# Thirty-two modulation tiles of layer two taken from TensorE's products to VectorE's multiply-and-sum

## The reference, cut to what matters

```
modulate(t, shift, scale) = t * (1.0 + scale) + shift
mod = silu(c) @ ada_w[layer] + ada_b[layer]      # six vectors of 1024 per layer
```

## Time and profile before

| | us |
|---|---|
| median of three runs | 1952.42 |
| the profiled execution | 1952.34 |
| its span, from the first to the last instruction | 1950.6 |
| TensorE busy | 1773.7 (91%) |
| VectorE busy | 823.5 (42%) |
| ScalarE busy | 355.2 (18%) |

### The profile page before, as it was taken

The page is one execution under the profiler, slowest core; times in us unless marked ns, Lnnn a source line. Parts: engine busy times, 40 slices in busy tenths (PEclk is TensorE's granted clock), DMA queues, the critical chain, the costliest instruction groups (busy, mean ns, idle before and its releaser), DMA issues.

```text
span 1950.6 us, 33854 instructions
## 1 busy us (share of the span) xinstructions
PE 1773.7 (91%) x14556; PEld 1372.6 (70%) x14556; DVE 823.5 (42%) x1796; ACT 355.2 (18%) x853; POOL 0.2 (0%) x4
## 2 busy tenths in 40 slices
PE   8999999999999999999999999999999766666666
PEld 4456644888888886777788887878788644555545
DVE  1355535766667325444444413268433111111112
ACT  0233313211110003222211102112332000000002
POOL 0000000000000000000000000000000000000000
PEclk9999999999999999999999999899999988988889
DMA  9455642222221305112333543132376999999996
GB/s 372 178 217 225 256 151 83 87 86 86 86 102 60 119 33 151 65 65 76 130 130 134 226 163 146 65 130 74 143 288 258 419 427 429 429 428 429 429 429 278
DMA packets 30925, 394.10 MB, mean 202 GB/s; under 512 B 3440, under 2 KB 6512, under 8 KB 8176
## 3 DMA queue, kind: packets, MB, share of 16 engines
q1 hardware_dynamic: 30832, 392.74, 50.2%
HBM read 391.68 MB, written 1.05 MB: 201 GB/s over the span
## 4 chain that ended last, share of the span: by engine, by line
PE 78%; DMA 19%; DVE 2%; ACT 1%; issue 1%; SPq 0%; DVEq 0%
PE bank L498 23%; DMA ring<-w_moe 18%; PE bank L1673 13%; PE bank L551 8%; PE bank L1405 6%; PE bank L1886 3%; PE bank L3103 2%; PE bank L783 2%; PE bank L694 2%; PE bank L1882 1%; PE bank L1080 1%; PE bank L2221 1%; PE bank L1284 1%; PE bank L1920 1%; PE bank L1056 1%; PE bank L1938 1%
## 5 line engine op out<-in xcount | busy, mean ns | idle before, releaser
L498 PE MATMUL bank<-layer_input,ring 128*128 128x256 f32 x1152 | 257.2, 384 | 1.1 <-DVE arena L2481 1.1
L498 PEld LDWEIGHTS bank<-layer_input,ring 128*128 128x128 f32 x1152 | 220.1, 193 | 34.1 <-issue 3.0
L3103 PE MATMUL bank<-ring,arena 128*32 128x128 f32 x1920 | 77.0, 327 | 55.7 <-DMA ring<-w_moe 55.4
L1673 PE MATMUL bank<-arena 128*128 128x256 f32 x504 | 115.6, 379 | 0.0
L3103 PEld LDWEIGHTS bank<-ring,arena 128*32 128x32 f32 x1920 | 66.0, 132 | 68.1 <-DMA ring<-w_moe 66.2
L1405 PE MATMUL bank<-arena,ring 128*128 128x256 f32 x480 | 107.0, 380 | 1.4 <-ACT arena L1496 1.4
L3220 DVE TENSOR_TENSOR arena<-arena,bank 128x128 f32<-128x128 f32 x32 | 9.2, 288 | 227.4 <-PE bank L3103 227.4
L1673 PEld LDWEIGHTS bank<-arena 128*128 128x128 f32 x504 | 95.8, 190 | 13.0
L1405 PEld LDWEIGHTS bank<-arena,ring 128*128 128x128 f32 x480 | 90.7, 190 | 15.4 <-ACT arena L1496 2.8
L551 PE MATMUL bank<-arena,ring 128*128 128x256 f32 x452 | 99.1, 380 | 0.8 <-DVE arena L2031 0.6
L551 PEld LDWEIGHTS bank<-arena,ring 128*128 128x128 f32 x452 | 85.5, 190 | 13.3 <-issue 1.0
(11 more groups left out here) (469 smaller groups left out, 2641.3 us busy)
## 6 DMA issues: line engine op xcount, KB each, us to landing
arena<-w_moe SPq DMA_DIRECT2D x46, 2048.0 KB, 26.5
ring<-w_moe SPq DMA_DIRECT2D x45, 2048.0 KB, 25.8
ring<-w_ffn_in SPq DMA_DIRECT2D x22, 2048.0 KB, 7.8
ring<-w_ada_late SPq DMA_DIRECT2D x16, 2560.0 KB, 10.4
ring<-w_ffn_out SPq DMA_DIRECT2D x8, 2816.0 KB, 9.5
ring<-w_proj SPq DMA_DIRECT2D x7, 3072.0 KB, 9.9
ring<-w_na_pair SPq DMA_DIRECT2D x8, 1536.0 KB, 6.5
arena<-w_ada_far SPq DMA_DIRECT2D x2, 2048.0 KB, 25.1
```

Source lines behind the costliest of these rows:

```text
L498: last = pe.matmul(out, a, b, start=(k == 0), stop=(k == len(lhs) - 1))
L1673: last = pe.matmul(out, w[:, k * P:(k + 1) * P], x[:, k, :], start=(start and k == 0), stop=(stop and k == 3), skip_group_check=True)
L3103: ins = eng.matmul(bank[x][group[q], 0:P], xe[:, k, SLOTS * e:SLOTS * e + SLOTS], weight(e, last, (x * KT + k) * FE + q * P, P), start=(k ...
```

## The change

- `ada_late` becomes 8 chunks of 6 tiles (before: 16 of 5), 48 tiles instead of 80. TensorE makes them in the MLA heads in one piece a pair, cut in two: the first 4 (even pair) or 5 (odd pair) of the eight slices k between `project` and `turn`, the rest between `turn` and `attend`. VectorE turns and adds the piece once a pair, behind the copies of `turned`.
- The last 32 tiles (gate of the attention, and shift, scale and gate of the feed-forward part, of layer two) are made by VectorE in the neighbourhood heads, for the latent column. For each tile one `tensor_tensor_reduce` over 128 partitions by 1024 elements multiplies the weights, laid out with the outputs on the partitions, by `silu(c)` repeated on all partitions, sums, and adds `ada_b`. The pairs take 0, 4, 4, 4, 5, 5, 5, 5 tiles; four stand between `normalize` and `na_turned`, a fifth behind `na_turned`.
- SP loads `c` (0.5 MB, repeated on 128 partitions) and sixteen chunks of 1 MB with two tiles each, through three buffers, between the pairs' weights. ScalarE applies `Silu` to the repeated `c` at the end of pair 0.
- At the end of the MLA heads one of three small additions of 1 to a scale vector is replaced by a memset; the addition is made at the start of `na_out`.

```diff
@@ -95,19 +95,24 @@
 VALUE_W = 768
 
 
-ADA_FIRST, ADA_TILES = 4 * 4, 5
+ADA_FIRST, ADA_TILES, ADA_CHUNKS = 4 * 4, 6, 8
+FAR_FIRST = ADA_FIRST + ADA_TILES * ADA_CHUNKS
+FAR_BUFFERS, FAR_EACH = 3, 2
+FAR_PER_PAIR = (0, 4, 4, 4, 5, 5, 5, 5)
+FAR_TILES = sum(FAR_PER_PAIR)
+FAR_LOADS = FAR_TILES // FAR_EACH
 MLA_PAIRS, MLA_QUADS = MLA_H // 2, MLA_H // 4
 MLA_QP = MLA_PAIRS * (QLT + KVT)
 OPEN_GROUPS = ((0, 1), (1, 2), (2, 4), (4, 6), (6, 8))
 OPEN_AT = ((0, 0, 2048), (0, 2048, 4096), (1, 0, 4096), (2, 0, 4096), (3, 0, 4096))
 STREAM = [("ada", 2, KT * 512), ("mla_v", 1, KVT * D),
-          ("ada_late", 16, KT * ADA_TILES * P), ("mla_o", 2, 4096),
+          ("ada_late", ADA_CHUNKS, KT * ADA_TILES * P), ("mla_o", 2, 4096),
           ("ffn_in0", 11, 4096), ("ffn_out0", 4, 5632),
           ("na_pair", NA_PAIRS, 3072), ("na_o", 2, 4096),
           ("ffn_in1", 11, 4096), ("ffn_out1", 4, 5632),
           ("proj", 7, 6144), ("branch", 1, 4096), ("w_out", 2, 4096),
           ("moe", EXPERTS, (2 * KT + 2 * FET) * FE), ("cmp", 1, 4096), ("branch_hg", 1, 4096), ("mla_qk", 1, (MLA_QP + MLA_QUADS * QLT) * P),
-          ("ada_far", 2, KT * 512), ("mla_in", 2, 3 * D)]
+          ("ada_far", 2, KT * 512), ("mla_in", 2, 3 * D), ("far", FAR_LOADS, FAR_EACH * D), ("far_c", 1, D)]
 UPS = 2 * KT * FE
 RESIDENT = EXPERTS - QUAD
 LAST = EXPERTS - 1
@@ -322,6 +327,9 @@
                 if name == "na_pair" and first == 1:
                     sp.wait_ge(self.sem("ffn0_up_used"), FT + 4)
                     self.load_biases(sp, slice(4, 16), self.rest_in)
+                    self.load_pairs(sp, load, g0)
+                    first = n
+                    break
                 first += 1
             sem, upto = CHUNK_USED[name]
             turns = (n - first) // 2
@@ -346,6 +354,37 @@
             sp.wait_ge(self.sem(ready), 1)
             sp.dma_start(out[:, t, :], self.result()[:, t, :]).then_inc(self.sem("result_out"), 16)
         sp.wait_ge(self.sem("result_out"), 32)
+
+    def far_c(self):
+
+        return self.ring[0][:, 4096:4096 + D]
+
+    def far_weights(self, b):
+
+        w = FAR_EACH * D
+        return self.B[:, 6400 + b * w:6400 + (b + 1) * w] if b < 2 else self.ring[1][:, 4096:4096 + w]
+
+    def load_far(self, sp, i):
+
+        b = i % FAR_BUFFERS
+        if i >= FAR_BUFFERS:
+            sp.wait_ge(self.sem("ada_used"), len(OPEN_GROUPS) + FAR_EACH * (i - FAR_BUFFERS + 1))
+        sp.dma_start(self.far_weights(b), self.W["far"][i]).then_inc(self.sem(f"far_in{b}"), 16)
+
+    def load_pairs(self, sp, load, g0):
+
+        sp.dma_start(self.far_c(), self.W["far_c"][0]).then_inc(self.cvec_in, 16)
+        for i in range(FAR_BUFFERS):
+            self.load_far(sp, i)
+        i, used = FAR_BUFFERS, 0
+        for u in range(NA_PAIRS):
+            if u + RING < NA_PAIRS:
+                sp.wait_ge(self.sem("na_proj_done"), u + 1)
+                load(u + RING, (g0 + u) % 2, g0 + u + RING)
+            used += FAR_PER_PAIR[u]
+            while i < min(FAR_LOADS, used // FAR_EACH + FAR_BUFFERS):
+                self.load_far(sp, i)
+                i += 1
 
     def load_biases(self, sp, heads, loaded):
         biases = self.N[:, :].rearrange("p (t h k) -> p t h k", t=2, h=16)
@@ -685,11 +724,11 @@
 
         return self.X[:, 3712:3712 + 32 * KT].rearrange("p (k c) -> p k c", k=KT)
 
-    def ada_product(self, pe, out, weights, width):
+    def ada_product(self, pe, out, weights, width, inner=(0, KT)):
 
         cs = self.silu()
         n = width // 4
-        for k in range(KT):
+        for k in range(*inner):
             for g in range(4):
                 last = pe.matmul(out[32 * g:32 * g + 32, 0:n], cs[:, k, :],
                                  weights[:, k * width + g * n:k * width + (g + 1) * n],
@@ -714,7 +753,8 @@
     def ada_rest(self, who, eng):
 
         if who == "dve":
-            for layer, m in ((0, 4), (1, 1), (1, 4)):
+            eng.memset(self.ADA[:, 1, 2 * KT:, :], 0.0)
+            for layer, m in ((0, 4), (1, 1)):
                 sc = self.ADA[:, layer, m * KT:(m + 1) * KT, :]
                 self.link(eng, who, eng.tensor_scalar(sc, sc, 1.0, None, ALU.add))
 
@@ -958,7 +998,7 @@
                 order += [("qp", n // 2)] * fresh + [("qn", n), ("kn", n)]
                 order += [("swap", n // 2), ("rot", n // 2)] * fresh
             if u >= 0:
-                order += [("ada", 2 * u), ("ada", 2 * u + 1), ("av", u)]
+                order += [("ada", u), ("av", u)]
         return {x: r for r, x in enumerate(order)}
 
     def mla_heads(self, who, eng):
@@ -1026,11 +1066,16 @@
             if n % 2 == 0:
                 rotate(n // 2)
 
-        def ada(c):
-            g = FIRST["ada_late"] + c
-            pe.wait_ge(self.w_loaded[g % 2], 16 * (g // 2 + 1))
-            b = claim(("ada", c))
-            self.ada_product(pe, b, self.ring[g % 2], ADA_TILES * P).then_inc(s["ada_rows"], 1)
+        def ada(u, part):
+
+            g, b = FIRST["ada_late"] + u, self.mla_turn(s, ("ada", u))[0]
+            half = 4 + u % 2
+            if part == 0:
+                pe.wait_ge(self.w_loaded[g % 2], 16 * (g // 2 + 1))
+                claim(("ada", u))
+            last = self.ada_product(pe, b, self.ring[g % 2], ADA_TILES * P, ((0, half), (half, KT))[part])
+            if part == 1:
+                last.then_inc(s["ada_rows"], 1)
 
         q, k, un, sw, kp = [v[x] for x in ("q", "k", "un", "sw", "kp")]
         half = [slice(64 * j, 64 * j + 64) for j in range(2)]
@@ -1107,9 +1152,9 @@
             scores(u)
             if u + 1 < MLA_PAIRS:
                 project(u + 1)
-            ada(2 * u)
+            ada(u, 0)
             turn(u)
-            ada(2 * u + 1)
+            ada(u, 1)
             attend(u)
 
     def mla_heads_dve(self, dve, s, v):
@@ -1192,9 +1237,8 @@
                 normalize(u, part)
             if fresh:
                 rotated((u + 1) // 2)
-            ada(2 * u)
             turned(u)
-            ada(2 * u + 1)
+            ada(u)
             attended(u)
 
     def mla_heads_act(self, act, s, v):
@@ -2020,11 +2064,25 @@
                 for n in (2 * h, 2 * h + 1):
                     dve.tensor_scalar(p[:, n, :], p[:, n, :], rc[:, n:n + 1], None, ALU.mult).then_inc(s["scaled"], 1)
 
+        def far(i):
+
+            g, e = i // FAR_EACH, i % FAR_EACH
+            dve.wait_ge(self.sem("open_silu_ready"), 3)
+            dve.wait_ge(self.sem(f"far_in{g % FAR_BUFFERS}"), 16 * (g // FAR_BUFFERS + 1))
+            w, at = self.far_weights(g % FAR_BUFFERS)[:, e * D:(e + 1) * D], FAR_FIRST - 6 * KT + i
+            dve.tensor_tensor_reduce(out=w, in0=w, in1=self.far_c(), scale=1.0, scalar=self.vec("ada_b", FAR_FIRST + i, 1),
+                                     op0=ALU.mult, op1=ALU.add, accum_out=self.ADA[:, 1, at, 1:2])\
+                .then_inc(self.sem("ada_used"), 1)
+
         queries(0)
         for u in range(NA_PAIRS):
             maxima(u)
             normalize(u)
+            for i in range(min(FAR_PER_PAIR[u], 4)):
+                far(sum(FAR_PER_PAIR[:u]) + i)
             self.na_turned(u, 0, s, v, dve, dve.tensor_copy, "pt_dve")
+            if FAR_PER_PAIR[u] > 4:
+                far(sum(FAR_PER_PAIR[:u]) + 4)
             if u + 1 < NA_PAIRS:
                 queries(u + 1)
             dve.wait_ge(s["o_done"], u + 1)
@@ -2058,9 +2116,16 @@
             if u + 1 < NA_PAIRS:
                 keys(u + 1)
             self.na_turned(u, 1, s, v, act, act.copy, "pt_act")
+            if u == 0:
+                act.wait_ge(self.cvec_in, 32)
+                act.activation(self.far_c(), self.far_c(), ACT.Silu).then_inc(self.sem("open_silu_ready"), 1)
 
     def na_out(self, who, eng):
         oT = self.na_views()["oT"].rearrange("p (k t) -> p k t", k=KT)
+        if who == "dve":
+            eng.wait_ge(self.sem("ada_used"), len(OPEN_GROUPS) + FAR_TILES)
+            sc = self.ADA[:, 1, 4 * KT:5 * KT, :]
+            self.link(eng, who, eng.tensor_scalar(sc, sc, 1.0, None, ALU.add))
 
         def sources(k):
             if k == KT - 1:
@@ -3495,7 +3560,9 @@
         return w.reshape(KT, P, chunks, tiles, 4, 32).transpose(2, 1, 0, 4, 3, 5).reshape(chunks, P, -1)
     first = [by_rows(w, lo, hi) for lo, hi in OPEN_GROUPS]
     W["ada"], W["ada_far"] = np.stack([np.concatenate(first[:2], 1), first[2]]), np.stack(first[3:])
-    W["ada_late"] = by_group(w[:, :, n:], ADA_TILES)
+    W["ada_late"] = by_group(w[:, :, n:FAR_FIRST * P], ADA_TILES)
+    W["far"] = w[:, :, FAR_FIRST * P:].reshape(D, FAR_LOADS, FAR_EACH, P).transpose(1, 3, 2, 0).reshape(FAR_LOADS, P, -1)
+    W["far_c"] = np.broadcast_to(a["c"][0], (1, P, D))
     w = a["mla_w_in"][0]
     pe = np.tile(w[:, QL + KVL:], (1, P // DR))
     w = np.concatenate([w[:, :QL + KVL], pe], 1).reshape(2, KT // 2, P, 6 * P)
```

## The result

The changed kernel takes **1941.57 us**, the median of 6 runs (1934.31 to 1941.98); the kernel before took 1951.91 us in the same comparison (6 runs, 1950.81 to 1955.59). The ratio is 0.9942 with a 95% interval from 0.9929 to 0.9955, so 11.3 us less, with bounds of 8.8 and 13.9 (the two medians differ by 10.3 us). One slow execution of one later kernel (pieces not cut, behind the `turn`), 2148.12 us at a mean granted clock of 0.83, is left out of that kernel's times.

What follows compares the result with a forecast made beforehand. TensorE was taken to bound both changed stages, VectorE costing only where TensorE waits. 1952.34 - 14.2 (MLA heads) + 0.3 + 0.1 (neighbourhood) = 1938.5 us; own range 1937.5 to 1940.5, whole range 1936.8 to 1945.5.

Steps and rivals of the forecast that it cites:

- rival B: MLA heads: shorter second part doesn't cover the copies, so attend waits 1.28 us in four odd pairs; 1943 us; chance 0.06.
- The piece of 192 columns: MLA heads: one piece of 2.74 us replaces two totalling 4.62 us, 1.88 us less a pair.
- Cutting it in two brings no further entry, because there were two entries before: MLA heads: cutting the 2.74 us piece adds no cost, so pairs 0 to 6 save 7 x 1.88 us.
- No wait of `turn` or `attend` in pairs 0 to 6: MLA heads: VectorE and ScalarE hold neither instruction, costed at nothing; margin in odd pairs 0.3 us.
- The last MLA pair: MLA heads, pair 7: shorter first part wins nothing before turn; attend then starts 1.04 us earlier.
- the small operations at the stage's end: End of MLA heads: a memset replaces a tensor_scalar one for one, costed at nothing.
- A tile: Neighbourhood heads: one VectorE multiply-and-sum takes 1.29 us, 1.2 us in a row; bounds 1.13 and 2.2 us.
- rival A: Neighbourhood heads: the multiply-and-sum runs at half rate, 2.2 us a tile, costing 6.9 us; 1945.1 us; chance 0.11.
- Rival C: Neighbourhood heads: tile over 2.5 us, slower than before; stalls 32p - 64.1 at p us a tile; chance 0.03.
- Pair 7 and `na_out`: Neighbourhood's end: four tiles delay the copies and attend by 0.3 us; na_out's added small tensor_scalar costs 0.1 us.
- The loads: SP's queue, neighbourhood heads: 17 added loads, 16.5 MB, add 100 GB/s to 68 and delay nothing.
- All of it carries to the end: Whole kernel: the stages' savings reach the end-to-end time in full, since no later stage waits for a fixed time.

Runs made afterwards that it cites:

- VectorE's part alone: Against the kernel before: TensorE still makes all 80 tiles in 16 pieces, VectorE makes its 32 once more with all loads; 1950.82 us, ratio 0.9998.
- the doubled tiles: Against the changed kernel: each VectorE tile computed twice, the first copy into a place nobody reads; 1953.47 us (one time), neighbourhood 223.27 us.

## Why the prediction was right

The median of 1941.57 us lies in the stated range, 1936.8 to 1945.5, but outside the forecast's own, 1937.5 to 1940.5, and nearer to rival B (1943) than to 1938.5. The total alone would not tell the two apart; the stages and the waits do.

**Which stage gives and which takes** came out as forecast: -13.53 us in the MLA heads (forecast -14.2), +0.18 in the neighbourhood (+0.4), and each part done alone gave its own term.

**The piece of 192 columns** is 2.74 us when it is not cut, exactly the two rows' slope. **"Cutting it in two brings no further entry, because there were two entries before" was the mis-sized term.** The count of entries is right, but the price was then taken from the wrong side: two pieces of 2.31 us hold two entries, and I subtracted one piece of 2.74 us, which holds one. Two parts are 2.87 us. From the stage's first matmul to the last pair's first piece it was 249.99 - 91.86 = 158.13 us and is 236.59 - 90.69 = 145.90: 12.23 less, which is 7 x 1.75 (4.62 - 2.87), where 7 x 1.88 = 13.16 was forecast. An MLA pair is 18.38 us, not 18.2.

**No wait of `turn` or `attend` in pairs 0 to 6**: right, and the cover is needed: with all of it taken away the stage took 4.6 us more. B needed a part of three slices to be too short, and it isn't.

**The last MLA pair**: 1.14 us less up to `attend`, forecast 1.04; the growth of the idle time before `turn` from 1.42 to 1.97 us is the shorter piece that wins nothing there. Behind it another 13.56 - 12.23 - 1.14 = 0.19 us went. That is the small operations at the stage's end, costed at nothing because they are one for one: VectorE's three additions took 0.58 us, two take 0.32, and the memset (0.11 us) lies under what is in front of it. TensorE's wait for them fell from 1.35 to 1.16 us, and with VectorE's part alone, which has two additions and no memset, to 1.14.

**A tile**: 1.279 us for 1.29, 1.21 in a row for 1.2. This ends rival A (2.2 us). The half-rate rule of the Trainium skill (Vector Engine (DVE) Microarchitecture Reference, Points that are easy to get wrong) is stated for the SCALAR_TENSOR_TENSOR shape with two non-bf16 SBUF sources. The row of just that shape contradicts it with 1285 ns, and the multiply-and-sum, another operation, also ran at 1.25 ns an element. Rival C's condition, over 2.5 us a tile, was false. Its formula names the right waits and is somewhat high: the doubled tiles cost 10.1 us of waits for 12.7 by the formula, and the other 2.8 us of the 12.9 came with the lower clock.

**Pair 7 and `na_out`**: 0.18 us in all, where 0.3 and 0.1 were forecast. `attend` stands at the end of the copies as forecast, a little earlier, and `na_out`'s added operation shows no price.

**The loads**: DMA in a neighbourhood pair rose from 68 GB/s to 159 in a pair with four tiles (100 more were forecast, 91 came) and to 204 in the pair with five. No tile waited for its weights: the 32 show no idle time before them.

**The total.** 13.35 us of changed stages against 13.8 in the sum leave 1939.0 us from the profiled 1952.34. That is 0.45 of the 3.1 us by which the forecast missed; the other 2.6 us lie outside the changed stages. "All of it carries to the end" is the step that is not borne out in full. Each median has to be set against that of the kernel before beside it: the three differences are 10.3, 11.7 and 11.35 us, 3.0, 1.7 and 2.0 us short of 13.35. Over all profiles the unchanged stages add up to 1561.6 to 1564.5 us in the kernel before and in the one with VectorE's part alone (three profiles), and to 1559.8 to 1567.4 in the ten of kernels with fewer pieces (means 1563.3 and 1564.5). Part of that spread comes in steps of 1.5 to 1.7 or 2.9 us where the granted clock is lower. Part does not: the opening stage took 89.7 to 92.2 us, always at a granted clock of 1.00, and the experts' stage 436.6 to 440.5 us at 0.87 or 0.88.

**What stays open.** The three intervals of the changed kernel in us are 8.8 to 13.9, 5.9 to 13.5 and 5.7 to 13.1. All have a middle 2 us or more below 13.35, and the last doesn't reach it. The four comparisons of kernels with uncut pieces point the same way: their changed stages save 14.1 to 15.5 us, their ratios 12.7 to 14.6 us. So some 2 us of the stages' saving seem to be lost elsewhere, though no single interval but the last shows it, and comparisons that share the runs of the kernel before are not independent. Whether the change makes the clock fall more often in later stages, makes another stage wait, or whether this is chance, the runs don't settle.

## What to carry to other kernels

When work is taken out of a stream of matmuls, price the pieces before and after with the same number of entries: split the price into a part per slice and a part per entry, and count what the instructions behind pay as well. Work put on an idle engine is free up to the next instruction that the busy engine waits for, gap by gap, not up to the engine's idle share; find the stage's last pair, since its gaps are shorter. And before a profile's total is read as a change's effect, compare the stages that didn't change: here they alone moved by up to 7.6 us. The reverse holds too: a saving read from the changed stages alone (13.35 us) can be more than the totals bear out (9.4 to 11.3 us by the three ratios).

## What the runs showed of the hardware

A run of the modulation's matmuls, which use 128-row, 32-column weight tiles, costs TensorE 0.13 us once, beside 0.325 us for each slice, and a `turn` of 24 transposes with 128x128 tiles takes 0.15 us more directly behind such a run than behind the projections (2.77 against 2.62 us). That the change of the tile's shape is the reason is a reading that no run tests by itself. After the same 1.97 us of idle time TensorE's granted clock stayed at 1.00 in one execution and fell to 0.50 during the next `turn` in another, at a cost of 1.5 us. The multiply-and-sum of 1024 fp32 elements from two SBUF sources takes VectorE 1279 ns (1.21 us from start to start in a row) and is followed by a read of the accumulator of 0.08 us, which lies under the next one.
